# A hybrid attention + MoE step on one core: branch A's scores alternate between key-value groups, branch C's odd heads write their keys to the upper partitions, and half a gate projection moves behind the keys

## The chip, the cores and the metric

The kernel runs on one core of one Trainium2 chip. The metric is the device time of one execution in microseconds. The kernel before took 1704.36 us, the median of three runs (1704.34 to 1705.16).

## The reference, cut to what matters

Two layers; each has a token-mixing and a mixture-of-experts sub-layer, for 128 context tokens and 128 latent tokens (T = 256 columns in all). All data are fp32.

```
z = h @ w_in                                   # (T, 1024) @ (1024, 5792)
A  oa = softmax_sink(qa ka^T / 8, sink) va     # 8 query heads of 64, 2 key-value heads: head h uses kv = h // 4
B  od = rms(softmax(q1 k1^T) v - lam * softmax(q2 k2^T) v)        # 4 heads, two maps each
C  kv = ckv @ w_ukv ; k = [k_nope(64), kpe(32)], v (64)           # 8 heads, ckv has rank 128
   om = softmax(qm k^T) v
merged = ga*(oa @ w_branch_a) + gb*(od @ w_branch_b) + gc*(om @ w_branch_c);  ga, gb, gc = sigmoid(h @ w_gate)
a = merged @ w_out
x = x + g1 * rms_norm(a)
scores = sigmoid(h2 @ router_w); top 6 of 64 experts; y = sum of gated SwiGLU experts + one shared expert
```

Context tokens see 128 keys, latent tokens 256 (cached or context keys, and their own).

## The kernel before, in words

Each engine has one program, written out by hand in its order; semaphores tie them together. All weights stream through a ring of 12 slots of 1 MB in SBUF, loaded by SyncE (L349, L360). A slot's load is issued when TensorE has released it (`release`), so TensorE's own progress starts the transfers. Per layer: modulation (L560), the input projections (L617, `project`), among them twelve jobs of gate columns (`gate_job`, 256 gate columns each, in two halves of 128, `parts`), small "prep" jobs that make the keys and values of the attention, 18 attention units, the branch projections (L856), w_out (L904), the router with the shared expert (L926 to L994, L946), and 32 pairs of experts (L1050 gate and up, L1076 down, L1099 combine, L510 transposes).

Prep jobs are counted by `prep_done` (TensorE) and `prep_ev` (VectorE, which copies each job's PSUM bank out). From job 5 on they rotate over five banks, 2 to 6 (`prep_bank`: job i uses bank 2 + i % 5 and waits until job i - 5 has been copied out). Jobs 11 and 12 are a rotary step of C's queries (three VectorE operations each, L1535 to L1537), job 13 the state outputs (L1593, L1594), jobs 14 to 21 C's keys, one head each (L768: 64 output channels by 384 tokens, copied out at L1597), jobs 22 to 24 C's values (L772, copied at L1600). Before the keys TensorE runs the whole of gate job 3.

The 18 units of the attention are six each of A, B and C; two of the six hold four heads with 128 keys (context), four hold two heads with 256 keys (latent). In step s TensorE runs the scores of unit s (L791 for A, L797 for B, L801 for C), half a gate job (L617, up to s = 15), the transposes of unit s - 1 (L510) and the weighted values of unit s - 2 (L842). A unit's scores lie in bank 2 + 2 (u % 2), B's two maps in that bank and the next. In A the heads of a unit follow each other with the same key-value head, so all matmuls of a unit read the same 64 partitions of the queries and keys. In B the two maps take turns between partitions 0-63 and 64-127.

An fp32 matmul stands in the trace as two records (two passes).

After the shared expert's first steps (`shared_gate_up(1, range(5))`) TensorE waits for the chosen experts `sel` of VectorE, computes ranks with five small matmuls, and finishes the shared expert. In the first expert pair, before the k = 2 step of the gate and up projection (L1050), TensorE transposes the token lists (L1032), once VectorE has found them (L1791 to L1796, eight rounds). From that, VectorE makes the row numbers, and GpSimd gathers the tokens of the pairs 1 and later (L498).

Of the kernel before, what the change touches and what calls it, by code (L numbers as in the profile page):

```python
# [26 lines left out]
ALU = mybir.AluOpType  # L27
# [3 lines left out]
P = 128  # L31
D = 1024
KC = D // P
# [99 lines left out]
def hybrid_layers(nc, a, o):  # L133
    with ExitStack() as ctx:
# [371 lines left out]
        def _(pe):  # L506
# [15 lines left out]
            for l in range(DEPTH):  # L522
# [238 lines left out]
                transpose(PS[:, b, 0:P], kA[:, 0:P])  # L761
                transpose(PS[:, b, P:2 * P], ckvT[:, 0:P])
                transpose(PS[:, b, 2 * P:2 * P + C_QK], kC[0:C_QK, 0, 0:P], C_QK).then_inc(prep_done, 1)
                gate_job(3)

                for h in range(C_HEADS):
                    b = prep_bank(14 + h)
                    pe.matmul(PS[0:C_NOPE, b, 0:384], w_ukv[:, h, 0:C_NOPE], ckvT, start=True, stop=True).then_inc(prep_done, 1)  # L768

                for t in range(3):  # L770
                    b = prep_bank(22 + t)
                    pe.matmul(PS[:, b, :], ckvT[:, t * P:(t + 1) * P], w_ukv[:, :, C_NOPE:C_NOPE + C_V],  # L772
                              start=True, stop=True).then_inc(prep_done, 1)


                def scores(u):
                    br, t, g = ATT[u]
                    b = 2 + 2 * (u % 2)
                    q0, k0, kn = t * P, t * P, P + t * P
                    if u < 2:  # L780

                        pe.wait_ge(prep_ev, l * PREP_JOBS + (21, 23)[u])
                    else:

                        pe.wait_ge(prob_exp, (l * UNITS + u - 1) * 4)
                    n = 4 if t == 0 else 2
                    for i in range(n):
                        if br == "A":
                            h = n * g + i
                            kv, c = h // 4, h % 4  # L790
                            last = pe.matmul(PS[:, b, i * kn:(i + 1) * kn], qA[HD * kv:HD * (kv + 1), c, q0:q0 + P],  # L791
                                             kA[HD * kv:HD * (kv + 1), k0:k0 + kn], start=True, stop=True)
                        elif br == "B":

                            j, m = divmod(i, 2)
                            h = (n // 2) * g + j
                            last = pe.matmul(PS[:, b + m, j * kn:(j + 1) * kn], qB[HD * m:HD * (m + 1), h, q0:q0 + P],  # L797
                                             kB[HD * m:HD * (m + 1), h, k0:k0 + kn], start=True, stop=True)
                        else:
                            h = n * g + i  # L800
                            last = pe.matmul(PS[:, b, i * kn:(i + 1) * kn], qC[0:C_QK, h, q0:q0 + P],  # L801
                                             kC[0:C_QK, h, k0:k0 + kn], start=True, stop=True)
                    last.then_inc(scores_done, 1)
# [11 lines left out]
                def weighted_values(u):  # L815
                    br, t, g = ATT[u]
                    pe.wait_ge(probT_ready, l * UNITS + u + 1)
                    if u >= 1:

                        pe.wait_ge(o_ready, l * UNITS + u)  # L820
                    heads = (2 if t == 0 else 1) if br == "B" else (4 if t == 0 else 2)

                    for kt in range(t + 1):
                        for i in range(heads):
                            h = heads * g + i
                            tile = kt + t
                            if br == "A":
                                v = vA[:, tile, (h // 4) * HD:(h // 4 + 1) * HD]
                            elif br == "B":
                                v = vB[:, tile, h * P:(h + 1) * P]  # L830
                            else:
                                v = vC[:, tile, h * C_V:(h + 1) * C_V]
                            if br == "B":
                                out = PS[:, 7, i * P:(i + 1) * P]
                            else:
                                out = PS[HD * (i % 2):HD * (i % 2) + HD, 7, (i // 2) * P:(i // 2 + 1) * P]
                            blk = i * (t + 1) + kt
                            weights = probT[:, u % 2, blk * P:(blk + 1) * P]
                            if br == "B":
                                last = pe.matmul(out, weights, v, start=(kt == 0), stop=(kt == t), skip_group_check=True)  # L840
                            else:
                                last = pe.matmul(out, v, weights, start=(kt == 0), stop=(kt == t), skip_group_check=True)  # L842
                    last.then_inc(pv_done, 1)
# [139 lines left out]
                logits(1)  # L983
                for half in range(2):
                    token_rows(1, half)
                shared_gate_up(1, range(5))

                pe.wait_ge(sel_ready, l + 1)
                pe.matmul(PS[:, 0, 0:N_EXPERTS], ones, sel[:, 0, :], start=True, stop=False)
# [5 lines left out]
                for t in range(2):  # L995
                    last = transpose(PS[0:N_EXPERTS, 1, P + t * P:P + (t + 1) * P], sel[:, t, :])
                last.then_inc(keys_tr, 1)
                shared_gate_up(1, range(5, KC))

                def first_tokens():  # L1000
                    for t in range(2):
# [18 lines left out]
                with pe.Fori(0, npass) as p:  # L1020
# [15 lines left out]
                    def gate_up(g):  # L1036

                        if g:
                            pe.wait_ge(xe_ready, done + (2 * g + 2))
                        for k in range(KC):  # L1040
                            if g == 0 and k % 4 == 0:
                                pe.wait_ge(xe_ready, done + (k // 4 + 1))
                            for e in range(2):
                                n = 6 * g + 2 * (k // 4) + e
                                if k % 4 == 0 and e == 0:
                                    arrived_pair(n, base)
                                if g == 0 and k == 2 and e == 0:
                                    transpose_lists()
                                w = ring[:, n % RING_SLOTS, :].rearrange("p (k c) -> p k c", k=4)
                                last = pe.matmul(PS[e * CAP:(e + 1) * CAP, 0, :], xe[:, k, e * CAP:(e + 1) * CAP], w[:, k % 4, :],  # L1050
                                                 start=(k == 0), stop=(k == KC - 1), skip_group_check=True)
                                if e == 0 and (k == 4 or (k == 0 and g >= 1)):
                                    release(last, 2)
                        last.then_inc(gu_done, 1)
# [83 lines left out]
        def _(act):  # L1138
# [11 lines left out]
            for l in range(DEPTH):  # L1150
# [72 lines left out]
                def exponentiate(u):  # L1223
# [8 lines left out]
                        act.activation(sinke[:, u % 2, 0:n], sinke[:, u % 2, 0:n], ACT.Exp).then_inc(sink_exp, 1)  # L1232
                    for i in range(n):
                        m, j = divmod(i, n // 2)
                        src = PS[:, b + m, j * kn:(j + 1) * kn] if br == "B" else PS[:, b, i * kn:(i + 1) * kn]
                        act.activation(prob[:, u % 2, i * kn:(i + 1) * kn], src, ACT.Exp,  # L1236
                                       scale=(C_QK if br == "C" else HD) ** -0.5, bias=negm[:, u % 2, i:i + 1],
                                       accum_out=psums[:, u % 2, i:i + 1]).then_inc(prob_exp, 4 // n)
# [129 lines left out]
        def _(dve):  # L1368
# [30 lines left out]
            for l in range(DEPTH):  # L1399
# [194 lines left out]
                ve.tensor_copy(state[:, 768:800], b[:, 2 * P + C_NOPE:2 * P + C_QK]).then_inc(prep_ev, 1)  # L1594
                for h in range(C_HEADS):
                    b = prep(14 + h)
                    ve.tensor_copy(kC[0:C_NOPE, h, :], b[0:C_NOPE, 0:384]).then_inc(prep_ev, 1)  # L1597
                for t in range(3):
                    b = prep(22 + t)
                    ve.tensor_copy(vC[:, t, :], b).then_inc(prep_ev, 1)  # L1600
# [1 line left out]
                def row_maxima(u):  # L1602
# [3 lines left out]
                    n, kn = (4, P) if t == 0 else (2, 2 * P)  # L1606
                    scale = (C_QK if br == "C" else HD) ** -0.5
                    m = negm[:, u % 2, 0:n]
                    if br == "B":
                        s = PS[:, b:b + 2, 0:(n // 2) * kn].rearrange("p m (j k) -> p m j k", k=kn)  # L1610
                        step(ve.reduce_max(m.rearrange("p (m j) -> p m j", m=2), s, X))
                    else:
                        step(ve.reduce_max(m, PS[:, b, :].rearrange("p (i k) -> p i k", k=kn), X))
                    if br == "A":

                        ns = nsink[:, n * g:n * g + n]
                        step(ve.scalar_tensor_tensor(out=m, in0=m, scalar=-scale, in1=ns, op0=ALU.mult, op1=ALU.min))
                        ve.tensor_tensor(sinke[:, u % 2, 0:n], m, ns, ALU.subtract).then_inc(negm_ready, 1)
                    else:
                        ve.tensor_scalar(m, m, -scale, None, ALU.mult).then_inc(negm_ready, 1)  # L1620

# [232 lines left out]
def pack_blocks(w):  # L1854

    out = np.zeros((DEPTH, LOADS, P, 2048), np.float32)
    for l in range(DEPTH):
# [16 lines left out]
        put(L_UQ, w["mla_w_uq"][l])  # L1874
        for j in range(10):
            put(L_GL + j, w_in[:, GL + 256 * (j + 2):GL + 256 * (j + 3)])
        for half in range(2):
            for b, name in enumerate(("w_branch_a", "w_branch_b", "w_branch_c")):
                put(L_BR + 3 * half + b, w[name][l][:, 512 * half:512 * half + 512])
        gate_up = np.concatenate([w["shared_w_gate"][l], w["shared_w_up"][l]], axis=1)  # L1880
        for rows in range(2):
            for half in range(2):
# [52 lines left out]
```

## Time and profile before

| What | us |
|---|---|
| median of three runs | 1704.36 |
| the profiled execution | 1704.68 |
| its span, first to last instruction | 1702.9 |
| TensorE (PE) busy | 1665.1 (98%) |
| VectorE (DVE) busy | 430.7 (25%) |
| ScalarE (ACT) busy | 324.8 (19%) |
| GpSimd (POOL) busy | 120.0 (7%) |
| weights' queue (q1), share of 16 DMA engines | 75.4% |

PE's busy time is time in which at least one matmul is under way; the ends of matmuls are modelled, and two matmuls on different parts of the array can be under way together. So the duration of one record says little of the pace; the start of the next group does.

### The profile page before, as it was taken

Reading aid. Unit: us, or ns where it says so; the run is one execution under the profiler, and the core shown is the slowest. Engines: PE = TensorE matmul, PEld = TensorE weight load, DVE = VectorE, ACT = ScalarE, POOL = GpSimd, SP = SyncE. Lnnn points to the kernel's source line nnn. Section 1 sums busy time; section 2 is a strip of 40 time slices with the busy share of each in tenths; the row PEclk is TensorE's granted clock in tenths of the full one; section 3 lists DMA queues with packets and bytes.
Section 4 is the critical chain, followed back from the end, with each engine's and each line's share of the span. In section 5 each row is a group of like instructions: output and inputs, shape, how many; then the busy total and the mean of one; then the engine's idle time right before and its main releaser. Section 6 shows DMA issues by size and latency. Waiting matters only on the chain. (4 is left out here: it accounts for less than half of the span.)

```text
span 1702.9 us, 21074 instructions
## 1 busy us (share of the span) xinstructions
PE 1665.1 (98%) x8107; PEld 892.7 (52%) x8107; DVE 430.7 (25%) x1183; ACT 324.8 (19%) x786; POOL 120.0 (7%) x164
## 2 busy tenths in 40 slices
PE   5999999999999999999999999999999999999998
PEld 3778788543333333333368878884433333333332
DVE  1114444361111111111131444543411111111112
ACT  1010341121111111111120113403111111111111
POOL 3001000020000000001020000001100000000000
PEclk9999999999999999999999999999999999999999
DMA  9994233379999999999999732235899999999993
GB/s 388 397 410 164 76 117 118 118 282 419 425 426 424 425 425 426 425 425 424 420 389 422 292 115 99 99 110 207 323 426 425 426 425 425 426 425 424 426 425 159
DMA packets 61100, 561.94 MB, mean 330 GB/s; under 512 B 13020, under 2 KB 13168, under 8 KB 21072
## 3 DMA queue, kind: packets, MB, share of 16 engines
q1 hardware_dynamic: 45504, 529.55, 75.4%
q0 software_dynamic: 15504, 31.09, 5.3%
q8 instruction: 66, 1.08, 0.3%
q14 instruction: 26, 0.21, 0.0%
HBM read 575.95 MB, written 6.88 MB: 342 GB/s over the span
## 5 line engine op out<-in xcount | busy, mean ns | idle before, releaser
L1050 PE MATMUL PS<-ring,region 128*64 128x512 f32 x2048 | 451.0, 592 | 0.7 <-ACT region L1331 0.7
L1050 PEld LDWEIGHTS PS<-ring,region 128*64 128x64 f32 x2048 | 146.4, 137 | 290.4 <-issue 290.3
L617 PE MATMUL PS<-region,ring 128*128 128x256 f32 x1088 | 245.3, 381 | 0.5 <-DMA ring<-in_blocks 0.5
L1099 PE MATMUL PS<-region 128*128 128x512 f32 x512 | 241.0, 594 | 0.0
L1076 PE MATMUL PS<-ring,region 128*64 128x512 f32 x1024 | 233.8, 598 | 0.2
L617 PEld LDWEIGHTS PS<-region,ring 128*128 128x128 f32 x1088 | 203.8, 190 | 34.2 <-issue 6.3
L1804 DVE SCALAR_TENSOR_TENSOR region<-region,PS 128x256 f32<-128x256 f32 x64 | 26.9, 421 | 662.8 <-ACT region L1338 662.8
L510 PEld LDWEIGHTS PS<-const,region 128*128 128x128 f32 (+1 forms) x925 | 106.5, 141 | 115.7 <-issue 67.3
L510 PE MATMUL PS<-const,region 128*128 128x128 f32 (+1 forms) x925 | 137.8, 278 | 15.7 <-DMA region<-in_c 9.6
L1076 PEld LDWEIGHTS PS<-ring,region 128*64 128x64 f32 x1024 | 67.7, 136 | 157.4 <-issue 156.7
L1344 ACT ACTIVATE region<-PS 128x512 f32<-128x512 f32 x128 | 76.4, 597 | 265.9 <-PE PS L1076 265.9
L1099 PEld LDWEIGHTS PS<-region 128*128 128x128 f32 x512 | 87.3, 190 | 65.6 <-issue 64.4
L498 POOL DMA_INDIRECT region<-h_table,region x62 | 61.3, 989 | 817.7 <-DVE region L1812 752.3
L1338 ACT ACTIVATE region<-PS 128x256 f32<-128x256 f32 x64 | 24.5, 384 | 406.0 <-PE PS L1050 406.0
L1331 ACT ACTIVATE region<-PS 128x512 f32<-128x512 f32 x128 | 76.2, 597 | 132.6 <-PE PS L510 132.6
L856 PE MATMUL PS<-region,ring 128*128 128x256 f32 x384 | 84.1, 380 | 0.0
L856 PEld LDWEIGHTS PS<-region,ring 128*128 128x128 f32 x384 | 72.6, 190 | 10.1 <-issue 0.3
L1812 DVE SCALAR_TENSOR_TENSOR region<-PS,region 64x256 f32<-64x256 f32 x128 | 61.9, 484 | 4.4
L904 PE MATMUL PS<-ring,region 128*128 128x512 f32 x128 | 55.6, 592 | 0.0
L560 PE MATMUL PS<-ring,condT 128*32 128x256 f32 x768 | 47.0, 394 | 6.7 <-DMA ring<-in_blocks 5.4
L1820 DVE TENSOR_SCALAR region<-const,region 128x256 f32<-128x256 f32 x64 | 22.6, 353 | 106.6 <-PE PS L1099 106.6
L1236 ACT ACTIVATE region<-PS,negm 128x128 f32<-128x128 f32 (+1 forms) x96 | 39.0, 415 | 34.8 <-issue 20.2
(270 smaller groups left out, 991.2 us busy)
## 6 DMA issues: line engine op xcount, KB each, us to landing
ring<-in_expert_blocks SPq DMA_DIRECT2D x192, 2048.0 KB, 17.1
ring<-in_blocks SPq DMA_DIRECT2D x120, 1024.0 KB, 19.6
region<-post_rows POOLq DMA_DIRECT2D x8, 512.0 KB, 6.2
h_first<-region POOLq DMA_DIRECT2D x4, 512.0 KB, 6.4
h_table<-region POOLq DMA_DIRECT2D x4, 512.0 KB
region<-in_w_kvk POOLq DMA_DIRECT2D x2, 640.0 KB, 18.6
region<-in_mla_w_ukv POOLq DMA_DIRECT2D x2, 512.0 KB, 21.8
region<-in_post_pack POOLq DMA_DIRECT2D x2, 512.0 KB, 25.4
```

The lines of the kernel that those rows point to most:

```text
L498: pool.indirect_dma_start(xg[:, g % XG, :] if g else xg[:, 0, 0:D], None, table if g else first_table, bass.IndirectOffsetOnAxis(ap=row_i[ ...
L510: return pe.transpose(out, in_, ident[0:n, 0:n])
L560: last = pe.matmul(PS[32 * g:32 * g + 32, MOD_BANK[group], half * 256:half * 256 + 256], condT[:, k, :], w[:, k % 2, 256 * g:256 * g + 256 ...
L617: last = pe.matmul(PS[:, j % 2, m * T:(m + 1) * T], w[:, k, m * P:(m + 1) * P], hT[:, k, :], start=(k == 0), stop=(k == KC - 1))
L856: last = pe.matmul(PS[:, b + n // 2, (n % 2) * T:(n % 2 + 1) * T], w[:, k, jj * P:(jj + 1) * P], src[:, k, :], start=(k == 0), stop=(k == 3))
L904: last = pe.matmul(PS[:, 4 + 2 * t + half, :], merged[:, k, t * P:(t + 1) * P], w[:, k % 4, :], start=(k == 0), stop=(k == KC - 1))
L1050: last = pe.matmul(PS[e * CAP:(e + 1) * CAP, 0, :], xe[:, k, e * CAP:(e + 1) * CAP], w[:, k % 4, :], start=(k == 0), stop=(k == KC - 1), s ...
L1076: last = pe.matmul(PS[e * CAP:(e + 1) * CAP, 2 + half, :], hid[:, f, e * CAP:(e + 1) * CAP], w[:, f, half * HALF:(half + 1) * HALF], start ...
L1099: last = pe.matmul(PS[:, 4 + 2 * t + half, :], hot[:, t * P:(t + 1) * P], og[:, half * HALF:(half + 1) * HALF], start=False, stop=True, sk ...
L1331: act.activation(xe[:, 4 * half:4 * half + 4, :].rearrange("p k s -> p (k s)"), bank(3 if g <= 1 and half else 1), ACT.Copy).then_inc(xe_r ...
L1344: act.activation(og[:, half * HALF:(half + 1) * HALF], bank(2 + half), ACT.Copy).then_inc(og_ready, 1)
L1812: ve.scalar_tensor_tensor(out=hid_rows[rows], in0=PS[rows, 0, 2 * P:4 * P], scalar=gate, in1=act_g[rows], op0=ALU.mult, op1=ALU.mult).then ...
```

## The change

- Branch A: a unit's matmuls alternate between key-value head 0 and 1 (partitions 0-63 and 64-127), each into a bank of its own, as in B. The heads of a unit are now slot (c, kv) with h = 4 kv + c; the rows of w_branch_a, the sinks and the blocks of the probabilities follow that order. Two waits on `prep_ev` grow by one, since unit 0 now writes banks 2 and 3, unit 1 banks 4 and 5.
- Branch C: odd heads' keys are written to PSUM partitions 64-127 and copied by VectorE down to SBUF partitions 0-63. Gate job 3 is split: its first half ahead of the keys, its second between keys and values.
- One more k step of the shared expert (six, not five) ahead of the wait for `sel`, and the transposes of the token lists at k = 3, not k = 2.

```
-                gate_job(3)
+                gate_job(3, (0,))
                 for h in range(C_HEADS):
                     b = prep_bank(14 + h)
-                    pe.matmul(PS[0:C_NOPE, b, 0:384], w_ukv[:, h, 0:C_NOPE], ckvT, ...)
+                    odd = h % 2 * C_NOPE
+                    pe.matmul(PS[odd:odd + C_NOPE, b, 0:384], w_ukv[:, h, 0:C_NOPE], ckvT, ...)
+                gate_job(3, (1,))
...
-                        pe.wait_ge(prep_ev, l * PREP_JOBS + (21, 23)[u])
+                        pe.wait_ge(prep_ev, l * PREP_JOBS + (22, 24)[u])
...
-                            h = n * g + i
-                            kv, c = h // 4, h % 4
-                            last = pe.matmul(PS[:, b, i * kn:(i + 1) * kn], qA[HD * kv:HD * (kv + 1), c, q0:q0 + P],
+                            j, kv = divmod(i, 2)
+                            c = (n // 2) * g + j
+                            last = pe.matmul(PS[:, b + kv, j * kn:(j + 1) * kn], qA[HD * kv:HD * (kv + 1), c, q0:q0 + P],
...
-                                v = vA[:, tile, (h // 4) * HD:(h // 4 + 1) * HD]
+                                v = vA[:, tile, (i % 2) * HD:(i % 2 + 1) * HD]
...
-                            blk = i * (t + 1) + kt
+                            blk = (i % 2 * (heads // 2) + i // 2 if br == "A" else i) * (t + 1) + kt
...
-                shared_gate_up(1, range(5))
+                shared_gate_up(1, range(6))
...
-                shared_gate_up(1, range(5, KC))
+                shared_gate_up(1, range(6, KC))
...
-                                if g == 0 and k == 2 and e == 0:
+                                if g == 0 and k == 3 and e == 0:
                                     transpose_lists()
...
-                    ve.tensor_copy(kC[0:C_NOPE, h, :], b[0:C_NOPE, 0:384]).then_inc(prep_ev, 1)
+                    odd = h % 2 * C_NOPE
+                    ve.tensor_copy(kC[0:C_NOPE, h, :], b[odd:odd + C_NOPE, 0:384]).then_inc(prep_ev, 1)
...
-                    if br == "B":
+                    if br in "AB":
                         s = PS[:, b:b + 2, 0:(n // 2) * kn].rearrange("p m (j k) -> p m j k", k=kn)
...
-                        ns = nsink[:, n * g:n * g + n]
+                        ns = nsink[:].rearrange("p (m c) -> p m c", m=2)[:, :, (n // 2) * g:(n // 2) * (g + 1)]
+                        m, e = (v.rearrange("p (m j) -> p m j", m=2) for v in (m, sinke[:, u % 2, 0:n]))
...
+        by_slots = w["w_branch_a"][l].reshape(A_KV, A_HEADS // A_KV, HD, -1).swapaxes(0, 1).reshape(A_HEADS * HD, -1)
```

## Rows read from the trace of the kernel before

**Rows 1.** The page: busy us of the engines (share of the span), instructions.

```profile
PE 1665.1 (98%) x8107; PEld 892.7 (52%) x8107; DVE 430.7 (25%) x1183; ACT 324.8 (19%) x786; POOL 120.0 (7%) x164
```

**Rows 2.** Groups by line and form: scores of A, B: busy us, mean ns, idle before.

```profile
L791 PE MATMUL PS<-region 64*128 64x256 f32 x32 | 9.0, 402 | 0.0
L797 PE MATMUL PS<-region 64*128 64x256 f32 x32 | 5.6, 428 | 0.0
```

**Rows 3.** Timeline, B's scores: start us, us, what, idle before and its releaser.

```profile
210.11 0.71 PE L797 MATMUL PS<-region 64*128 64x128 f32 x8
210.75 3.72 PE L617 MATMUL PS<-region,ring 128*128 128x256 f32 x16
```

**Rows 4.** Timeline of layer 0 from gate job 3 to behind unit 0's scores.

```profile
162.17 7.10 PE L617 MATMUL PS<-region,ring 128*128 128x256 f32 x32
166.06 0.19 DVE L1594 COPY region<-PS 128x32 f32<-128x32 f32 x1
169.19 5.37 PE L768 MATMUL PS<-region 128*64 128x384 f32 x16
170.09 5.06 DVE L1597 COPY region<-PS 64x384 f32<-64x384 f32 x8 [3.84 <-PE PS L768]
174.50 2.84 PE L772 MATMUL PS<-region 128*128 128x512 f32 x6
177.27 1.16 PE L791 MATMUL PS<-region 64*128 64x128 f32 x8
178.35 3.72 PE L617 MATMUL PS<-region,ring 128*128 128x256 f32 x16
```

**Rows 5.** The instructions of L1597: duration in ns, min/median/max.

```profile
L1597 DVE COPY region<-PS x16: 549/550/551, 170.1 to 1010.2; 64x384 f32<-64x384 f32 x16
```

**Rows 6.** The chain of waits, layer 1's experts: start us, us, what.

```profile
1221.14 6.87 PE PS L1050 x32
```

**Rows 7.** Timeline, router to first expert pair, layer 0.

```profile
352.18 4.46 PE L946 MATMUL PS<-ring,region 128*128 128x512 f32 x10
357.44 0.43 PE L989 MATMUL PS<-sel,const 128*128 128x64 f32 x2 [0.80 <-DVE sel L1740]
360.11 0.98 DVE L1758 TENSOR_SCALAR region<-const,ranks,sel 128x64 f32<-128x64 f32 x4
361.60 0.51 PE L1002 MATMUL PS<-const,region 128*128 128x2 f32 x4
370.96 1.94 PE L1050 MATMUL PS<-ring,region 128*64 128x512 f32 x8 [0.34 <-ACT region L1331]
373.32 0.30 PE L1032 MATMUL PS<-const,region 64*64 64x32 f32 x4 [0.43 <-DVE region L1793]
379.54 0.66 PE L510 MATMUL PS<-const,region 128*128 128x128 f32 x4 [0.61 <-DMA region<-h_table,region]
380.99 0.84 PE L510 MATMUL PS<-const,region 128*128 128x128 f32 x6 [0.79 <-DVE region L1812]
```

**Rows 8.** The same stretch of layer 1, its end.

```profile
1206.71 1.94 PE L1050 MATMUL PS<-ring,region 128*64 128x512 f32 x8 [0.34 <-ACT region L1331]
1208.79 0.30 PE L1032 MATMUL PS<-const,region 64*64 64x32 f32 x4
1215.25 0.66 PE L510 MATMUL PS<-const,region 128*128 128x128 f32 x4 [0.85 <-DMA region<-h_table,region]
1216.56 0.84 PE L510 MATMUL PS<-const,region 128*128 128x128 f32 x6 [0.65 <-DVE region L1812]
```

**Rows 9.** DMA issues, KB, us to landing: 380 to 400, then 800 to 850.

```profile
ring<-in_expert_blocks SPq DMA_DIRECT2D x4, 2048.0 KB, 10.1
...
ring<-in_expert_blocks SPq DMA_DIRECT2D x5, 2048.0 KB, 22.3
```

**Rows 10.** Window: length, PE, PEld, DVE, ACT, POOL busy, clock, DMA share, GB/s.

```profile
365.00:370.00 5.00, 5.00 (x16) 2.32 (x15) 3.83 (x14) 0.01 (x1) 0.27 (x1) 1.00 0.14 35
```

**Rows 11.** TensorE's waits, 850 to 900 us: us in total, times, longest.

```profile
PE PS L560 <- DMA ring<-in_blocks: 0.7, 1, 0.7
```

More of the change, by code:

```diff
@@ L763, in _ @@
                 transpose(PS[:, b, 2 * P:2 * P + C_QK], kC[0:C_QK, 0, 0:P], C_QK).then_inc(prep_done, 1)
-                gate_job(3)
+                gate_job(3, (0,))
                 for h in range(C_HEADS):
                     b = prep_bank(14 + h)
-                    pe.matmul(PS[0:C_NOPE, b, 0:384], w_ukv[:, h, 0:C_NOPE], ckvT, start=True, stop=True).then_inc(prep_done, 1)
+                    odd = h % 2 * C_NOPE
+                    pe.matmul(PS[odd:odd + C_NOPE, b, 0:384], w_ukv[:, h, 0:C_NOPE], ckvT, start=True, stop=True).then_inc(prep_done, 1)
+                gate_job(3, (1,))
                 for t in range(3):
@@ L1234, in exponentiate @@
                         m, j = divmod(i, n // 2)
-                        src = PS[:, b + m, j * kn:(j + 1) * kn] if br == "B" else PS[:, b, i * kn:(i + 1) * kn]
+                        src = PS[:, b + m, j * kn:(j + 1) * kn] if br in "AB" else PS[:, b, i * kn:(i + 1) * kn]
                         act.activation(prob[:, u % 2, i * kn:(i + 1) * kn], src, ACT.Exp,
@@ L1614, in row_maxima @@
                     if br == "A":
-                        ns = nsink[:, n * g:n * g + n]
+                        ns = nsink[:].rearrange("p (m c) -> p m c", m=2)[:, :, (n // 2) * g:(n // 2) * (g + 1)]
+                        m, e = (v.rearrange("p (m j) -> p m j", m=2) for v in (m, sinke[:, u % 2, 0:n]))
                         step(ve.scalar_tensor_tensor(out=m, in0=m, scalar=-scale, in1=ns, op0=ALU.mult, op1=ALU.min))
-                        ve.tensor_tensor(sinke[:, u % 2, 0:n], m, ns, ALU.subtract).then_inc(negm_ready, 1)
+                        ve.tensor_tensor(e, m, ns, ALU.subtract).then_inc(negm_ready, 1)
                     else:
@@ L1876, in pack_blocks @@
             put(L_GL + j, w_in[:, GL + 256 * (j + 2):GL + 256 * (j + 3)])
+        by_slots = w["w_branch_a"][l].reshape(A_KV, A_HEADS // A_KV, HD, -1).swapaxes(0, 1).reshape(A_HEADS * HD, -1)
         for half in range(2):
-            for b, name in enumerate(("w_branch_a", "w_branch_b", "w_branch_c")):
-                put(L_BR + 3 * half + b, w[name][l][:, 512 * half:512 * half + 512])
+            for b, matrix in enumerate((by_slots, w["w_branch_b"][l], w["w_branch_c"][l])):
+                put(L_BR + 3 * half + b, matrix[:, 512 * half:512 * half + 512])
         gate_up = np.concatenate([w["shared_w_gate"][l], w["shared_w_up"][l]], axis=1)
```

## The prediction

> **What bounds the kernel now.** I read the page's busy times first: TensorE works 98% of the span, every other engine a quarter or less [rows 1]. So what counts is time on TensorE, and any wait that a shorter TensorE part uncovers. Then I read the groups by line and form, for what a unit of scores costs in A and in B, whose shapes are the same [rows 2]; the timeline of the stretch that the change rebuilds, for which instruction follows which and how far VectorE is behind [rows 3, 4]; the timeline from the router to the first pair of experts, where TensorE waits in several places for tenths of a microsecond [rows 7, 8]; and last the DMA views, since the expert stage streams weights without a pause [rows 9 to 11].
>
> A profiled TensorE record ends when its pipeline ends, so I take paces from one group's start to the next group's start, or from busy time that is a union.
>
> **Part 1: the scores of branch A.** B has the alternating order already. A latent unit (two heads, 256 keys) of A keeps TensorE busy 9.0 / 8 = 1.13 us, one of B 5.6 / 8 = 0.70 us: four such units in each of two layers [rows 2]. Gain 0.43 us each, 3.4 us in all. A context unit (four heads, 128 keys) takes 178.35 - 177.27 = 1.08 us in A [rows 4] and 210.75 - 210.11 = 0.64 us in B [rows 3]. Gain 0.44 us, four units, 1.8 us. **Sum 5.2 us.** All of it is on the path, since gate halves follow at once. Below this the bound is nothing (if A does not pair), above it 12 x 1.1 / 2 = 6.6 us (every unit halved); I take the B rows because the instructions have the same form. VectorE's maximum over two banks and the small operations on the sinks in two rows keep their size; they run while TensorE works on 3.7 us of gate half [rows 4], and B lives with the same order.
>
> What is late next: the units follow each other 0.43 us sooner, but the time from a unit's scores to its transposes is as before, because the half gate projection in between is as before. In B the same engines hold that rhythm. The waits that grow to 22 and 24 concern job 21's and job 23's copies. The first is examined below; the second is wanted a whole unit later. Cost nothing.
>
> **Part 2: branch C's keys.** Before, from the start of gate job 3 to the end of unit 0's scores, TensorE needs 178.35 - 162.17 = 16.18 us: gate 7.02, keys 5.31 (16 passes of 0.32 and a little), values 2.77, scores 1.08 [rows 4]. Passes in two column halves do run side by side in this kernel: the expert rows have 32 passes of 512 columns in 6.87 us, 0.215 us each, against 0.32 us for a pass of only 384 columns here, which is 0.43 us for 512 [rows 4, 6]. A head's second pass then runs beside the next head's first, so 16 passes want nine slots of 0.32 = 2.9 us.
>
> VectorE does not follow that fast. Its copy takes 0.55 us [rows 5], and copies come at between 0.55 (no gap) and 0.65 us (the rate of the keys before, 5.06 us for eight [rows 4]); I take 0.59. Counted from the first key's start, the first copy starts at 0.9 (170.09 - 169.19, [rows 4]). Five banks: the eighth key needs the third copy, done at 0.9 + 3 x 0.59 = 2.67, and starts at about 2.8. It ends 0.65 later, so the keys take 3.45 us. The keys now start 3.5 us sooner, at 162.17 + 3.51 = 165.68. The fifth one waits for the state copies, which end at 166.25 [rows 4], 0.57 after the start; its turn comes at 1.3, so this is no wait. But that cover was 2.9 us and is now 0.7.
>
> The second half of the gate job (3.5 us) then hides the last copies: the eighth is done at 0.9 + 8 x 0.59 = 5.6, the first scores are wanted at 3.45 + 3.5 + 2.77 = 9.7. New total: 3.51 + 3.45 + 3.51 + 2.77 + 0.64 = 13.88, and 0.1 for leaving and entering the column mode beside the gate twice. 16.18 - 13.98 = 2.2 us, of which 0.44 is unit 0 and counted in part 1. **1.8 us a layer, 3.6 us in all.** Bounds: nothing, if the column halves do not pair; 5.31 - 2.9 = 2.4 a layer if VectorE keeps up. No row shows a copy that reads partitions 64-127 and writes 0-63. Its duration I bound by the same copy in place, 0.55 us, and by twice that; even at 1.1 us four odd copies add 2.2 us, of which the third copy (one odd ahead of it) puts 0.55 on the path. I take 0.55, the row it is nearest to.
>
> The Trainium skill (TensorE: Matmul & The Clock Gate, Part 3, "What overlaps and what doesn't") says that a weight load overlaps with running matmuls only when the row group differs. By that rule the keys, which all use all 128 rows, would gain little, and the sum would be 5.2 + 1.1. The expert rows have the same row group and show the pace of two at once [rows 6], so here the trace disagrees and I keep the pairs; the rule is a rival below.
>
> **Part 3: one more step of the shared expert ahead of the wait for sel.** A step is two passes, about 0.86 us (x10 in 4.46 with its tail, [rows 7]). TensorE sat idle 0.80 us before the ranks' matmul at 357.44. The step fills this and makes that matmul 0.06 late, which VectorE, busy until long after, does not notice. Two steps are left behind it where there were three: TensorE is at the first tokens' matmuls 0.80 us sooner, at 360.80, but their operand comes from L1758, which ends at 361.09 [rows 7]. With some 0.1 to get through, they start at 361.18 where it was 361.60. **0.42 us** for all that follows: the row number, the lists on VectorE (they begin behind the first row), the first gather, and TensorE's own queue, so gate and up of pair 0 starts at 370.54.
>
> **Part 4: the lists' transposes at k = 3.** A k step of gate and up is four passes, 0.86 us. In layer 1, where no wait for the lists is listed, TensorE came to them at 1208.79, 0.36 behind two steps from 1206.71 [rows 8]: so much it costs to leave the column mode; I take 0.3. In layer 0 it waited 0.43 us for them [rows 7]. Now the lists are ready 0.42 sooner, at 372.90, and TensorE comes to them at 370.54 + 3 x 0.86 + 0.3 = 373.42, 0.10 later than before, without a wait. What hangs on them is the gather of pair 1, 379.54 - 373.32 = 6.22 us later [rows 7]: TensorE could transpose its rows from 379.64 to about 380.2. The hidden rows' chain hangs on the end of gate and up: 373.42 + 0.24 + 5 x 0.86 = 377.96, where it was 373.32 + 0.24 + 6 x 0.86 = 378.72; its transposes stood 2.27 us behind that, so now 380.23. They start at 380.25 instead of 380.99: **0.75 us** for parts 3 and 4 in layer 0. In layer 1 gate and up starts at 1206.29, the lists' turn is 1209.17 (0.38 later than before), the gather lands at 1215.63, and the hidden transposes start at about 1216.2 instead of 1216.56 [rows 8]: **0.35 us**. Bounds for both layers together: 1.5 above (2 x 0.42, the wait of 0.43 and some 0.2 of the switch), and -0.3 below, if the gathers land 0.7 us later still in each.
>
> **Sum:** 5.2 + 3.6 + 1.1 = 9.9 us. The profiled execution took 1704.68, 1.8 outside its span of 1702.9; it becomes 1694.8. It stood 0.3 above the median, so the median becomes 1694.5.
>
> **Rivals.** (a) *Keys do not pair*, by the rule named above or since each waits for its copy: part 2 gives nothing, 1698.1. The expert rows speak against it. (b) *The weights' stream keeps its time.* An expert load's way from issue to landing grows from 10.1 to 22.3 us in layer 0 [rows 9], so the DMA engines are a little slower than TensorE, and at the start of layer 1 TensorE does wait for weights, 0.7 us [rows 11]. If the stream doesn't begin sooner when TensorE does, layer 0's share (2.6 + 1.8 + 0.75 = 5.15) comes back as waits there: 1699.6. Against it: just before the experts the DMA engines are idle, share 0.14 [rows 10], with the ring full; the loads are released by TensorE, so the stream moves with it. (c) *A does not pair*, so the change doesn't do there what it says: 1699.7. Only something in A that B lacks could do it. (d) *Slower: the odd heads' copies.* If moving 64 partitions down were slow, the odd copies would hold up the last keys, the values and VectorE's queue, in which unit 0's maxima stand behind them. Some 4.1 us a layer are hidden (9.7 - 5.6). The whole gain of 4.95 a layer is gone at (4.1 + 4.95) / 4 = 2.3 us extra for each odd copy, four times its duration in place; at 3.2 us extra the kernel would take 1704.4 + 2 x (4 x 3.2 - 9.05) = 1711.9. Nothing in the trace speaks for such a price.
>
> **How the numbers follow.** Forecast 0.74, (a) 0.09, (b) 0.08, (c) 0.05, (d) 0.04. The likeliest gives 1694.5; its own bounds are 1692.7 (keys at 2.4 a layer, parts 3 and 4 at 1.5, 0.2 more in A) to 1696.7 (parts 3 and 4 nothing, the doubled copy 0.55 a layer). The range for 8 in 10 takes in (a) and ends at 1698.6; its low end, 1692.2, leaves 0.5 for A's units. A change below 0.2% (3.4 us) could not be told from none: faster than 1701.0 are all cases but (d) and mixtures of (b) with (a) or (c): 0.93; within, 0.04; slower, 0.03.
>
> **What would show it.** L791's busy time falls to about 8.5 us over both forms, and a context unit to 0.64 us. From gate job 3's start to behind unit 0's scores it is 14.0 us; the keys take 3.4, L1597 runs at below 0.6 us a copy and TensorE's last keys wait for it. The wait at L989 is gone, the one at L1032 too, and the wait for the gather of pair 1 has grown to over 1 us. Layer 1 begins 5.15 us sooner with a wait for weights still below 1 us. Wrong would be a wait for weights of several us at that place, keys of 5 us, or a stop in A's units that B doesn't have.

## The result, and the profile after

The changed kernel took 1708.33 us (median of 13 runs, 1707.30 to 1711.01), the kernel before in the same series 1704.91 (13 runs, 1704.03 to 1707.27). The ratio is 1.002, 95% interval 1.0012 to 1.0029: slower by 3.4 us, where 9.9 us less were forecast. The profiled execution took 1708.33 with a span of 1706.5.

Three of the four parts did what was forecast, nearly to the tenth. First the groups by line and form in the changed kernel (busy us, mean ns, idle before), branch A's scores (L793), branch C's keys (L769):

```profile
L769 PE MATMUL PS<-region 128*64 128x384 f32 x32 | 7.1, 502 | 0.0
L793 PE MATMUL PS<-region 64*128 64x256 f32 x32 | 5.6, 428 | 0.0
L793 PE MATMUL PS<-region 64*128 64x128 f32 x32 | 2.9, 297 | 0.0
```

A's latent units fell from 9.0 to the 5.6 us of B [rows 2], and both forms together are at the 8.5 us that the prediction gave as a sign. The timeline of the rebuilt stretch, layer 0, against [rows 4]:

```profile
161.93 3.64 PE L617 MATMUL PS<-region,ring 128*128 128x256 f32 x16
165.50 3.53 PE L769 MATMUL PS<-region 128*64 128x384 f32 x16
168.96 3.72 PE L617 MATMUL PS<-region,ring 128*128 128x256 f32 x16
172.52 2.74 PE L774 MATMUL PS<-region 128*128 128x512 f32 x6
175.19 0.71 PE L793 MATMUL PS<-region 64*128 64x128 f32 x8
175.83 3.72 PE L617 MATMUL PS<-region,ring 128*128 128x256 f32 x16
```

From gate job 3 to behind unit 0's scores it takes 175.83 - 161.93 = 13.90 us, forecast 13.98; before, 16.18. And the odd heads' copies down cost nearly what the copies in place cost (the instructions of L1600, odd and even heads together, duration in ns, min/median/max):

```profile
L1600 DVE COPY region<-PS x16: 549/554/560, 166.4 to 1008.2; 64x384 f32<-64x384 f32 x16
```

So TensorE comes to the first pair of experts 4.99 us sooner than before (365.97, where it was 370.96 [rows 7]; forecast 4.82). Of this, 0.24 us stood already at the start of gate job 3 (161.93 against 162.17), ahead of every edit, so the change itself gave 4.75. All of that and more is lost while the first pair is worked on. The timeline of TensorE there:

```profile
365.97 2.79 PE L1052 MATMUL PS<-ring,region 128*64 128x512 f32 x12 [0.34 <-ACT region L1333]
368.69 0.30 PE L1034 MATMUL PS<-const,region 64*64 64x32 f32 x4
368.93 4.51 PE L1052 MATMUL PS<-ring,region 128*64 128x512 f32 x20
380.12 2.40 PE L510 MATMUL PS<-const,region 128*128 128x128 f32 x10 [6.68 <-DMA region<-h_table,region]
382.45 5.26 PE L1078 MATMUL PS<-ring,region 128*64 128x512 f32 x16
387.54 7.03 PE L1052 MATMUL PS<-ring,region 128*64 128x512 f32 x32
```

The wait for the gather of pair 1's tokens, 0.61 us before [rows 7], is 6.68 us. Layer 1 has the same, 6.80 us, where it was 0.85 [rows 8]; first before, then after:

```profile
1217.48 3.65 PE L1076 MATMUL PS<-ring,region 128*64 128x512 f32 x16
1220.97 7.04 PE L1050 MATMUL PS<-ring,region 128*64 128x512 f32 x32
...
1203.82 2.79 PE L1052 MATMUL PS<-ring,region 128*64 128x512 f32 x12 [0.34 <-ACT region L1333]
1218.09 2.40 PE L510 MATMUL PS<-const,region 128*128 128x128 f32 x10 [6.80 <-DMA region<-h_table,region]
1220.42 4.41 PE L1078 MATMUL PS<-ring,region 128*64 128x512 f32 x16
1224.66 7.03 PE L1052 MATMUL PS<-ring,region 128*64 128x512 f32 x32
```

The rest of the loss is the clock: TensorE stands still from 373.4 to 380.1. The windows (length, busy of PE, PEld, DVE, ACT, POOL, granted clock, DMA share, GB/s):

```profile
370.00:375.00 5.00, 3.44 (x17) 0.86 (x12) 1.03 (x3) 0.38 (x1) 2.00 (x2) 1.00 0.86 305
375.00:380.00 5.00, 0.00 (x0) 0.00 (x0) 0.36 (x1) 0.00 (x0) 0.99 (x1) 0.55 0.83 338
380.00:382.00 2.00, 1.88 (x9) 1.88 (x10) 0.29 (x1) 0.60 (x1) 0.00 (x0) 0.50 0.14 47
...
384.00:386.00 2.00, 2.00 (x8) 0.62 (x6) 0.00 (x0) 0.00 (x0) 0.00 (x0) 0.57 0.92 393
386.00:388.00 2.00, 2.00 (x12) 0.59 (x10) 0.00 (x0) 0.84 (x2) 0.00 (x0) 1.00 1.03 442
```

The granted clock falls to 0.50, the lower level of 1.2 GHz, at about 375.5, while TensorE stands still, and is back at 1.00 at about 385.7, after 5.6 us of work. The 16 records of L1078 need 387.54 - 382.45 = 5.09 us to the next group; at full clock, before, the same 16 came in 385.40 - 381.92 = 3.48:

```profile
381.92 3.65 PE L1076 MATMUL PS<-ring,region 128*64 128x512 f32 x16
385.40 7.04 PE L1050 MATMUL PS<-ring,region 128*64 128x512 f32 x32
```

**Why the gather is late.** GpSimd issues it, and SyncE issues a 2 MB load of expert weights near it. Before (the two engines' timelines put together, layer 0):

```profile
375.22 1.01 POOL L498 DMA_INDIRECT region<-h_table,region  x1 [9.95 <-DVE region L1799]
376.54 0.34 SPq L360 DMA_DIRECT2D ring<-in_expert_blocks  x1
```

After:

```profile
370.32 1.01 POOL L498 DMA_INDIRECT region<-h_table,region  x1 [9.69 <-DVE region L1803]
371.05 0.34 SPq L360 DMA_DIRECT2D ring<-in_expert_blocks  x1
```

Before, the load came 0.31 us behind the end of the gather's 1.01 us of issue; now it comes 0.28 us ahead of that end. The load is released by TensorE at step k = 4 of the first gate and up. The lists used to be transposed at k = 2, in layer 0 behind a wait of 0.43 us, two steps ahead of the release; now only one step lies between. From its issue to TensorE's first use the gather takes 380.12 - 370.32 = 9.80 us, where it was 4.32. The difference, 5.5 us, is near the 4.9 us that 2 MB (2.1 million bytes) take at the 425 GB/s of the expert stage. That was my theory after reading the traces; the runs below test it.

### The profile page after: what moved, and what is told of

Read it like the earlier page. It is cut to its first block and busy times, and to the rows that moved or that the text cites. A ratio compares the mean times of both kernels' runs of the same rounds, so it can differ in the third digit from the quotient of the medians.

```text
span 1706.5 us, 21074 instructions
## 1 busy us (share of the span) xinstructions
PE 1660.3 (97%) x8107; PEld 888.0 (52%) x8107; DVE 431.1 (25%) x1183; ACT 324.8 (19%) x786; POOL 120.5 (7%) x164
## 5 line engine op out<-in xcount | busy, mean ns | idle before, releaser
L1078 PE MATMUL PS<-ring,region 128*64 128x512 f32 x1024 | 236.2, 603 | 0.0
L1078 PEld LDWEIGHTS PS<-ring,region 128*64 128x64 f32 x1024 | 68.3, 138 | 159.2 <-issue 158.5
```

The lines of the kernel that those rows point to most:

```text
L1078: last = pe.matmul(PS[e * CAP:(e + 1) * CAP, 2 + half, :], hid[:, f, e * CAP:(e + 1) * CAP], w[:, f, half * HALF:(half + 1) * HALF], start ...
```

## The experiments

Each run's time stands beside runs of the kernel before in the same series: 1704.96 us (median of 8) for lists_k2, before_k3, late_release and lists_k2_five, 1705.39 us (median of 15) for release_k5, release_early, branch_a_only and branch_c_only. The ratios are to these, with 95% intervals.

**lists_k2: the lists at k = 2 again, all else as changed.**

```
-                                if g == 0 and k == 3 and e == 0:
+                                if g == 0 and k == 2 and e == 0:
```

> The changed kernel with one edit undone: the token lists are transposed at k = 2 again, as before. Order theory (the gather of pair 1 loses 6 us a layer because SyncE's next 2 MB weight load, released at k = 4, is now issued 0.3 us ahead of the end of the gather's issue and not 0.3 us behind it): the gather is issued about 0.8 us sooner, ahead of the weights, lands about 4.3 us after its start, and the time falls to 1695, 10 us below the kernel before. Rival (the DMA engines are more crowded there because everything comes sooner, whatever the order of the two): the gather still lands 9 to 10 us after its start and the time stays at 1706 to 1708.

1696.46 us, ratio 0.9947 (0.9931 to 0.9964): 8.5 us faster than before, 12 faster than the changed kernel. The order is the old one and the landing is the old one, 375.32 - 370.99 = 4.33 us:

```profile
370.99 1.01 POOL L498 DMA_INDIRECT region<-h_table,region  x1 [9.59 <-DVE region L1803]
372.31 0.34 SPq L360 DMA_DIRECT2D ring<-in_expert_blocks  x1
375.32 0.66 PE L510 MATMUL PS<-const,region 128*128 128x128 f32 x4 [0.61 <-DMA region<-h_table,region]
```

The gather and the load both come over 4 us sooner than in the kernel before (375.22 and 376.54), and the gather still takes its old time; so it isn't the earlier hour by itself that costs. This is the fastest version that ran, though late_release below can't be told from it.

**before_k3: the kernel before, lists at k = 3, nothing else.**

```
-                                if g == 0 and k == 2 and e == 0:
+                                if g == 0 and k == 3 and e == 0:
```

> The kernel before with one edit: the lists are transposed at k = 3. Order theory: the gather's issue ends some 0.5 us later, behind the weight load, so it lands 5 to 6 us later in each layer and the kernel takes 1714 to 1717. Rival (it takes the shorter attention as well to crowd the transfers): within 1 us of 1704.9.

1718.35 us, ratio 1.0077 (1.0061 to 1.0094), a little above the range expected. One digit costs 13.4 us without any of the other edits. TensorE's waits in layer 1, 1160 to 1230 us, the longest:

```profile
PE PS L510 <- DMA region<-h_table,region: 7.0, 1, 7.0
```

**late_release and release_k5: lists at k = 3 as changed, pair 0's first slots released later.**

```
-                                if e == 0 and (k == 4 or (k == 0 and g >= 1)):
+                                if e == 0 and (k == (6 if g == 0 else 4) or (k == 0 and g >= 1)):
```

(release_k5 has a 5 for the 6.)

> The changed kernel, lists at k = 3 as changed, but pair 0 releases its first two ring slots at k = 6 and not at k = 4, so the weight load is issued some 1.7 us later. Order theory: the gather is ahead again, its landing takes 4.3 us, the time is 1695. Rival (the lists themselves are too late for the gather, or the transfers are crowded): the wait for the gather stays above 6 us and the time near 1708.

> The changed kernel, lists at k = 3, pair 0's first slots released at k = 5, 0.86 us later than changed and 0.86 sooner than in late_release. The weight load should come some 0.6 us behind the end of the gather's issue. Order theory: 1696 to 1697, as with k = 6. If the load must stay away for longer than the gather's issue, or the lists at k = 3 are too late in themselves: between 1698 and 1708.

late_release: 1696.92 us, ratio 0.9957 (0.9942 to 0.9971). release_k5: 1698.46 us, 0.9958 (0.9942 to 0.9973). The two ratios are the same, but the median of release_k5 is outside the 1696 to 1697 of the order theory and just inside the rival's 1698 to 1708. What decides is its trace. The gather is fast in both layers, and some 1.5 us of the profiled execution lie elsewhere: at the start of layer 1 the granted clock was 0.50 from about 864.8 to 868.2, and a group of twenty transposes needed 4.65 us to the next, where it was 3.14. Layer 0 of release_k5:

```profile
370.87 1.01 POOL L498 DMA_INDIRECT region<-h_table,region  x1 [9.68 <-DVE region L1803]
372.46 0.34 SPq L360 DMA_DIRECT2D ring<-in_expert_blocks  x1
375.29 1.61 PE L510 MATMUL PS<-const,region 128*128 128x128 f32 x10 [1.30 <-DMA region<-h_table,region]
```

The lists are as late as in the changed kernel, only the weight load is moved, and the gather is back at 4.42 us. So the lateness of the lists in itself costs no more than the 1.2 to 1.7 us of wait a layer that these two runs show; the prediction had foreseen that this wait grows to over 1 us.

**release_early: the kernel before, lists at k = 2, the load released one matmul sooner.**

```
-                                if e == 0 and (k == 4 or (k == 0 and g >= 1)):
+                                if e == (g == 0 and k == 3) and (k == (3 if g == 0 else 4) or (k == 0 and g >= 1)):
```

> The kernel before, the lists at k = 2, the only edit that pair 0's first two ring slots are released behind k = 3's second matmul, 0.4 us sooner than at k = 4. The weight load should then be issued 0.1 us ahead of the end of the gather's issue in both layers (it was 0.3 us behind). Order theory, with the end of GpSimd's issue as the point that decides: the gather lands behind the load, 1714 to 1718. If the point lies earlier in the gather's issue: unchanged, 1705. Rival (lateness of the lists, not order): unchanged, 1705.

1717.32 us, ratio 1.0066 (1.005 to 1.0081), inside the range expected. The edit moved the load further than expected: counted from the first gate and up, it is issued 4.73 us later (376.28 - 371.55), where it was 5.58 (376.54 - 370.96), so 0.85 us sooner and not 0.4, and 0.53 us ahead of the end of the gather's issue and not 0.1. So the run tests the order, and not where in the gather's issue the step lies. It is the counterpart of late_release: the lists are not touched at all, TensorE's own work neither, and the 12 us appear:

```profile
375.80 1.01 POOL L498 DMA_INDIRECT region<-h_table,region  x1 [9.95 <-DVE region L1799]
376.28 0.34 SPq L360 DMA_DIRECT2D ring<-in_expert_blocks  x1
...
385.22 2.40 PE L510 MATMUL PS<-const,region 128*128 128x128 f32 x10 [5.71 <-DMA region<-h_table,region]
```

A weight load issued *sooner* makes the kernel slower. For all kernels, the load's issue counted from the start of the gather's issue, and the gather's time until TensorE uses it, both in us, in layer 0 and layer 1:

| kernel | load after gather, layer 0 | gather to use, layer 0 | load after gather, layer 1 | gather to use, layer 1 | time, us |
|---|---|---|---|---|---|
| release_early | 0.48 | 9.42 | 0.51 | 10.31 | 1717.32 |
| before_k3 | 0.73 | 9.69 | 0.76 | 10.11 | 1718.35 |
| changed | 0.73 | 9.80 | 0.76 | 9.92 | 1708.33 |
| before | 1.32 | 4.32 | 1.35 | 4.56 | 1704.91 |
| lists_k2 | 1.32 | 4.33 | 1.35 | 4.56 | 1696.46 |
| lists_k2_five | 1.32 | 4.35 | 1.35 | 5.21 | 1697.49 |
| branch_c_only | 1.32 | 4.34 | 1.35 | 5.32 | 1701.63 |
| branch_a_only | 1.33 | 4.39 | 1.35 | 5.28 | 1699.97 |
| release_k5 | 1.59 | 4.42 | 1.62 | 4.67 | 1698.46 |
| late_release | 2.46 | 4.37 | 2.48 | 4.83 | 1696.92 |

Between 0.76 and 1.32 us the gather's time jumps by over 4 us. On either side it moves by less than 1 us, though not by nothing: in layer 1 the same 1.35 us go with 4.56 to 5.32, which the order of the two doesn't explain. The gather's issue lasts 1.01 us, so its end is a likely place for the step, but no run lies between.

**lists_k2_five: lists at k = 2 and five steps of the shared expert ahead, so A's and C's edits alone.**

```
-                shared_gate_up(1, range(6))
+                shared_gate_up(1, range(5))
...
-                shared_gate_up(1, range(6, KC))
+                shared_gate_up(1, range(5, KC))
```

> The changed kernel with the lists at k = 2 and five steps of the shared expert ahead of the wait for sel, as before: what is left are branch A's and branch C's edits. The prediction's parts 1 and 2 give 8.8 us: 1696. The run with six steps should be 0.5 to 1 us below it. Rival (the margin between gather and weight load is so thin that the sixth step alone tips it in one of the layers): the two kernels differ by 5 us or more.

1697.49 us, ratio 0.9952 (0.9936 to 0.9969). Against lists_k2 the median is 1.0 us higher, where part 3 forecast 0.84, but the intervals overlap, so the time doesn't show it. The trace shows the mechanism: the wait of 0.8 us for `sel` is back (TensorE's waits, layer 0):

```profile
PE PS L991 <- DVE sel L1744: 0.8, 1, 0.8
```

From the shared expert's last group ahead of that wait to the first gate and up it takes 366.65 - 347.86 = 18.79 us here and 366.74 - 348.31 = 18.43 in lists_k2, so the sixth step is worth 0.36 us a layer (in layer 1 1198.48 - 1179.69 = 18.79 and 1198.74 - 1180.31 = 18.43). The margin was not so thin that the sixth step tips it.

The times of this kernel hold something else as well. In its profiled execution TensorE waited 1.50 us for layer 1's gather, the granted clock fell to 0.50 behind that, and the 16 records of L1078 needed 1214.43 - 1209.25 = 5.18 us, where they are 3.48 in lists_k2:

```profile
1210.00:1212.00 2.00, 2.00 (x8) 0.69 (x6) 0.00 (x0) 0.00 (x0) 0.18 (x1) 0.50 0.98 350
```

**branch_a_only and branch_c_only: the kernel before with one branch's edits, as in the diff above.**

> The kernel before with branch A's edit alone. The prediction's part 1: twelve units at 0.43 us, 5.2 us less: 1699.7. Rival (TensorE is ahead, but the stream of weights is not, so part of layer 0's share comes back as waits for weights at the start of layer 1): 1700.5 to 1702, with those waits grown beyond the 0.7 and 0.2 us of before.

> The kernel before with branch C's edit alone (odd heads' keys on the upper partitions, half a gate job behind the keys). The prediction's part 2: 1.8 us a layer, 3.6 us less: 1701.3; VectorE's copies at 0.55 us for odd heads as for even ones. Rival (the copies down are slower, or the column halves do not pair): 1704 or more, and keys that take 5 us.

branch_a_only: 1699.97 us, ratio 0.9967 (0.9955 to 0.9979), 5.4 us less (forecast 5.2; the interval is 3.6 to 7.7 us). branch_c_only: 1701.63 us, ratio 0.9978 (0.9968 to 0.9987), 3.8 us less (forecast 3.6; 2.2 to 5.5). Both rivals on the array, that A or the keys do not pair, are out. Together the two gain 9.2 us alone and 7.5 in lists_k2_five, which has both; its interval, 5.3 to 10.9 us, holds both numbers, and 1.7 us of slow L1078 stand in its trace. The rival on the weights' stream shows nothing in branch_a_only, whose wait there is 0.6 us. It leaves a trace in branch_c_only: TensorE's waits for weights at the start of layer 1, 850 to 900 us.

```profile
PE PS L560 <- DMA ring<-in_blocks: 0.9, 1, 0.9
...
PE PS L647 <- DMA ring<-in_blocks: 0.5, 1, 0.5
```

That is 1.4 us, where it was 0.7 and 0.2. In lists_k2 it is 2.0:

```profile
PE PS L560 <- DMA ring<-in_blocks: 1.1, 1, 1.1
PE PS L647 <- DMA ring<-in_blocks: 0.9, 1, 0.9
```

## Why the prediction was wrong, by its steps

**Part 1 (branch A)** was right: 5.2 us forecast, 5.4 measured alone (3.6 to 7.7), and busy times equal to B's to the tenth.

**Part 2 (branch C)** was right: 3.6 forecast, 3.8 measured alone. The column halves pair although their row group is the same, the copies come at VectorE's pace, and moving 64 partitions down cost some 0.56 us (the single records of odd heads take 558 to 560 ns) against 0.55. From gate job 3 to the shared expert's last group ahead of `sel` layer 0 takes 347.54 - 161.93 = 185.61 us, where it was 352.18 - 162.17 = 190.01: 4.40 us less, and parts 1 and 2 forecast 2.6 + 1.8. The rule weighed there is that of the Trainium skill (TensorE: Matmul & The Clock Gate, Part 3), that a weight load overlaps with running matmuls only when the row group differs. What I had drawn from it, no gain in part 2, did not come: eight heads' keys took 3.46 us, where they took 5.31, with the same row group for all.

**Part 3 (the sixth step)** was right in the trace: the wait for `sel` is gone, and the step gave 0.36 us a layer by lists_k2 against lists_k2_five, where 0.42 was forecast. Times alone don't show it.

**Part 4 (the lists at k = 3)** is where it failed, in one sentence: "What hangs on them is the gather of pair 1, 379.54 - 373.32 = 6.22 us later". I took the time from lists to gathered rows as fixed, a property of the gather. In these runs it is near that only where the gather's issue has ended ahead of the next weight load's. I had moved the lists and had moved gate and up, each by its own amount, and had not asked what the release at k = 4 does, which is TensorE's as well and moves with gate and up. The rows for it could be had: the load's issue at 376.54, 0.31 us behind the end of the gather's. Gate and up without its stop brings the release forward by 5.49 us, the gather comes forward by only 4.90, and 0.31 turns into -0.28. The lower bound for the part, -0.3 us, allowed the gather 0.7 us more a layer; it was 5.5 in layer 0 and 5.4 in layer 1.

**What it cost.** The waits for the gather and for the hidden rows were 0.61 + 0.79 and 0.85 + 0.65 us in the two layers [rows 7, 8]; now they are 6.68 and 6.80, and none for the hidden rows: 10.6 us more. The lower clock adds 5.09 - 3.48 = 1.6 us on L1078 in layer 0 and 0.75 in layer 1 (1224.66 - 1220.42 = 4.24, before 3.49), and on the ten transposes some 0.75 us each time (2.33 us to the next group, where before it was 381.92 - 379.54 = 2.38 with 0.79 of it a wait): about 4 us in all. Against the parts 1 to 3 (8.8 + 0.84) and the 0.43 us of wait for the lists this makes about 4.5 us slower; the profiled executions differ by 3.65. A shorter way to the same: from the first gate and up to that of the second pair it took 14.44 and 14.26 us in the two layers (385.40 - 370.96 and 1220.97 - 1206.71), now 21.57 and 20.84, so 13.7 us more. Undone by one digit, the 12 us come back (lists_k2).

**The rivals.** (a), (c) and (d) did not happen. (b), the stream of weights that keeps its own time, may be true in a small part: in lists_k2 the waits for weights at the start of layer 1 are 2.0 us, 1.1 more than before, where the prediction's sign said below 1 us. That lists_k2 gains 8.5 us and not the 9.6 of parts 1 to 3 would fit, but its interval, 6.1 to 11.8 us, holds both. The kind of rival that decided was missing: a transfer that a faster TensorE starts sooner and that gets ahead of one on which the path hangs. In my sum the weight load had a price only as something that arrives, never as something that stands in the way.

**How the gather and the load share the engines.** The packets of the two queues tell part of it: q1 has the weights, q0 the gathers (packets, MB, share of the 16 engines). Before, 376.5 to 379.5 us:

```profile
q1 hardware_dynamic: 50, 0.57, 59.7%
q0 software_dynamic: 144, 0.21, 27.9%
```

The changed kernel, 371.5 to 379.0, then 379.0 to 381.0:

```profile
q1 hardware_dynamic: 154, 2.11, 68.8%
q0 software_dynamic: 238, 0.27, 17.1%
...
q0 software_dynamic: 194, 0.28, 37.8%
q1 hardware_dynamic: 8, 0.02, 2.1%
```

Before, the 0.2 MB that were wanted came while the load was only beginning. Now the whole load, 2.1 MB, goes through in the same 7.5 us as the first half of the gathers' bytes, and the other half comes behind it. So the gather neither waits until the load is over nor comes through beside it: it shares the engines and is done only about when the load is. In release_early, where the load is issued 0.48 us behind the gather's start, q0 moved nothing at all from 377.0 to 380.5, and q1 1.05 MB.

**What stays open.** Where the step lies between 0.76 and 1.32 us; why the load's packets get in first when it is issued ahead of the end of the gather's issue; and how far the delay goes with the size of the load (5.1 to 5.5 us more in layer 0, against 4.9 us for 2 MB at the stage's rate), since no run changed that size. The packets of pair 1's gather can't be told from those of the gathers issued behind it.

## What to carry to other kernels

When two DMA queues feed one path, a small urgent transfer and a large one that is not urgent, write down which is issued first and by how much, and recompute that margin for every edit that moves either, above all for edits that only take out a stop of the engine that releases the large one. Here 0.6 us of shift on a margin of 0.3 cost 12 us. The cheap cure is to release the large load one or two steps later, which cost nothing that these runs can tell, or to leave the work that the small one hangs on where it is even if it seems to stop the engine.

## What the runs showed of the hardware that was not expected

- A gather by GpSimd's queue (about 0.2 MB) is used 4.3 to 5.3 us after its issue began when the 2 MB load of the other queue is issued 1.32 us or more behind that start, and 9.4 to 10.3 us when it is issued 0.48 to 0.76 us behind. The separate queue doesn't protect it.
- TensorE stood still for 6.7 us; the granted clock was 0.50 from 375.5 to 385.7, also over the first 5.6 us of the work that followed, and L1078 took 5.09 us in place of 3.48. The two waits cost over a third more than their own length (4 us on 10.6). A short stop can cost it too: in lists_k2_five the clock fell behind a wait of 1.50 us, while waits of 1.57, 1.61 and 1.71 us at the same place in branch_a_only, branch_c_only and late_release left it at 1.00.
- The copies from partitions 64-127 to 0-63 cost nearly the same as those in place: 558 to 560 ns and 549 to 551 ns for 64 x 384 fp32.
